# Two of the three split operand forms of the channel mixer kept unsplit in HBM, their parts made after loading

## The chip, the cores and the metric

The kernel runs on 1 core of one Trainium2 chip. The metric is the device time of one execution in microseconds (us); for the kernel before it is 2160.81 us, the median of 3 runs (2160.64 to 2161.2). Products of TensorE take float32 operands that are written as a sum of two parts, "hi" (rounded to the type fp32r) and "lo" (the rest, also fp32r); each product is hi x hi + hi x lo + lo x hi.

## The reference, cut to what matters

The kernel computes one step of a one-layer encoder (an RG-LRU branch and an mLSTM branch, merged, then a channel mixer) for 1024 prompt columns and 64 sample columns, so 1088 columns. The change touches only the channel mixer:

```python
hmlp = jax.nn.relu(rmsnorm(x, norm_mlp) @ w_up)      # D_MODEL 1024 -> D_FF 4096
x = x + (hmlp * hmlp) @ w_down                       # D_FF 4096 -> D_MODEL 1024
```

## The kernel before, in words

The first two thirds of the program (to about 1449 us) are the branches and their merge. The channel mixer follows. It is cut into **groups** of 1024 hidden rows: up groups 0 to 3 (normed x times w_up), then down groups 4, 5 and 6 (squared hidden rows of up groups 0, 1 and 2 times w_down); the hidden rows of up group 3 are multiplied at the very end by other code (`last_x`, `last_term`). Each group has 4 **units** (r = 0 to 3) of 256 output rows. Within a unit the 2 x 2 block product is made with 7 block products instead of 8 (Winograd's form of Strassen's method). The 7 operands on the x side are B11, T1, T2, B21, T3, B22, T4, each 512 rows x 544 columns; B are blocks of x, T are sums and differences of blocks. TensorE (`unit`, line 1184 on) takes the products in the order P5, P6, P2, P7, P1, P3, P4, whose operands are T1, T2, B21, T3, B11, B22, T4; the P1 in a unit is already that of the next unit. So at a change of group ("transition") B11 of the new group is wanted first, in the last unit of the old group, then T1, T2, B21, T3, B22, T4. "Half" below means two of an operand's four 128-row blocks; TensorE waits for operands that are made on the chip half by half (`by_pair`).

The operands of the down groups are made from hidden rows in the up groups and stored in HBM (`forms_d`). ScalarE squares two of a unit's four hidden quarters, VectorE the other two. VectorE then makes the three sums T1, T2, T4 (`hid_sums`, `last_sum`), ScalarE their hi parts (`sum_hi`), VectorE their lo parts in place (`sums_lo`), and `store` writes four quarters of B and T3, three lo parts and three hi parts with four DMAs from ScalarE's queue. So B11, T3, B21 and B22 are stored whole (list `RAW`), T1, T2 and T4 as hi and lo (list `SPLIT`).

At the end of groups 3, 4 and 5, and at the start of the next, the next group's operands are loaded into the same 7 operand buffers (`form[f][part]`), each as soon as TensorE has done the last product that reads the old contents. A whole form is one DMA (`load_raw`) of 1088 KB, after which ScalarE makes hi in two instructions (`raw_hi`) and VectorE makes lo in place in two (`raw_lo`); a split form is two DMAs (`load_split`) and nothing more. Before the change ScalarE's queue in the last unit (r = 3) runs: hi of B11 and the load of T1 after step 1, the load of T2 after step 2, of B21 after step 3, of T3 after step 4, hi of B21 and the load of B22 after step 6; and in unit 0 of the next group hi of T3, hi of B22 and the load of T4. A queue is in order: an instruction that waits holds all behind it.

Two other jobs share the queues there. ScalarE makes the hi part of each weight form (`w_form`) into one of 4 slots, once TensorE has done the product four before; GpSimd combines the weight blocks (`combine`, line 795) and makes the lo parts (`lo`, line 792), 11 instructions of 128 x 512 per unit, all of them from on-chip memory to on-chip memory. ScalarE copies P1 out of its bank (`copy1`, into `snap`). VectorE empties the other banks: `partials` (P6, P5), `quarter` and `direct` (P2, P7 twice, P3, P4), `mixed` adds a quarter to `acc` in groups 5 and 6. TensorE may start a product only when the bank four products back is empty: P7 of a unit waits for the P4 of the unit before to be emptied. In group 3 ScalarE's `relu2` on the quarter of P7 comes between `w_form` and the load of T3 (step 4), and VectorE's lo of B21 and T3 stand ahead of the emptying of P4 (`hid21`).

Of the kernel before, what the change touches and what calls it, by code (L numbers as in the profile page):

```python
# [137 lines left out]
RAW, SPLIT = (B11, B21, T3, B22), (T1, T2, T4)  # L138
# [30 lines left out]
STORED_HI = 3  # L169
KEPT = FORMS + 3  # L170
UNIT_STORES = 64
# [40 lines left out]
def build(nc, x_t, small_d, rowmask_d, w_d, c0_d, rows_d, mixa_d, y_d, conv_d, hlast_d, c_d, n_d, m_d):  # L212
# [114 lines left out]
    def quarters(t, first, n):  # L327
# [5 lines left out]
    hid_h = [(quarters(acc_flat, 3 + 9 * j, 2), quarters(stage[:].rearrange("p a c -> p (a c)"), 4 + j, 1))  # L333
             for j in range(2)]
# [971 lines left out]
    def _(act):  # L1306
# [418 lines left out]
        def store(group, r):  # L1725

            act.wait_ge(h_step, FORMS * (4 * group + r) + 7)
            th, t_hi2 = hid_h[r % 2]
            for src, first, n in ((hid_q[r % 2], 0, 4), (hid_t[r % 2], 4, 3), (th, 7, 2), (t_hi2, 9, 1)):
                dst = forms_d[bass.ds(KEPT * group + first, n)][:, :, r, :]  # L1730
                act.dma_start(dst.rearrange("f p c -> p f c"), src).then_inc(h_st[r % 2], 16)
# [16 lines left out]
        def sum_hi(group, r, i):  # L1748

            u, (th, t_hi2) = 4 * group + r, hid_h[r % 2]  # L1750
            if i == 0:
                for stored_hid, count in hid_free(group, r):
                    act.wait_ge(stored_hid, count)
            act.wait_ge(h_step, FORMS * u + (1, 3, 4)[i])
            a((th[:, i, :] if i < 2 else t_hi2[:, 0, :]).bitcast(F32R), hid_t[r % 2][:, i, :], ACT.Copy, h_hi)
# [110 lines left out]
        def hid(group, r, prev, late_sums=(1, 2, 3)):  # L1866

            def between(step):
                if step in late_sums[0:3]:
                    for i in range(3):  # L1870
                        if late_sums[i] == step:
                            sum_hi(*prev, i)
                if step == 4:
                    relu2(group, r, 0)
                    relu2(group, r, 1)
                elif step == 5 and isinstance(group, int) and group == 0 and r in (1, 2):
                    norm_out(r)
                elif step == 6:
                    store(*prev)
            return between  # L1880
        for r in range(1, 4):
            unit(0, r, hid(0, r, (0, r - 1), (1, 2, 3)))
# [23 lines left out]
        def operands(group, r, step):  # L1906

            v = group - UP_GROUPS + 2
            if v <= DOWN_GROUPS:
                if (r, step) == (2, 5):  # L1910
                    load_raw(v, 0)
                elif (r, step) == (3, 1):
                    raw_hi(v, 0)
                    act.wait_ge(s_mm, index(group, r, P5) + 1)
                    load_split(v, T1)
                elif (r, step) == (3, 2):
                    act.wait_ge(s_mm, index(group, r, P6) + 1)
                    load_split(v, T2)
                elif (r, step) == (3, 3):
                    act.wait_ge(s_mm, index(group, r, P2) + 1)  # L1920
                    load_raw(v, 1)
                elif (r, step) == (3, 4):
                    act.wait_ge(s_mm, index(group, r, P7) + 1)
                    load_raw(v, 2)
                elif (r, step) == (3, 6):
                    raw_hi(v, 1)
                    act.wait_ge(s_mm, index(group, r, P3) + 1)
                    load_raw(v, 3)
# [19 lines left out]
            if (r, step) == (0, 0) and v > 1:  # L1948
                raw_hi(v - 1, 2)
            if (r, step) == (0, 1) and v > 1:  # L1950
                raw_hi(v - 1, 3)
# [43 lines left out]
    def _(dve):  # L1995
# [609 lines left out]
        def hid_sums(group, r):  # L2605
# [7 lines left out]
            dve.wait_ge(h_step, FORMS * u + 1)  # L2613
            dve.wait_ge(h_sq, 4 * u + 4)
            hid_combine(q[1], q[3], q[1], ALU.subtract)
            dve.wait_ge(h_step, FORMS * u + 2)
            hid_combine(t[:, 1, :], q[1], q[0], ALU.add)

        def last_sum(group, r):
# [3 lines left out]
            dve.wait_ge(h_step, FORMS * u + 3)  # L2623
            hid_combine(t[:, 2, :], q[2], t[:, 1, :], ALU.subtract)

        def sums_lo(group, r):
            u, t, (th, t_hi2) = 4 * group + r, hid_t[r % 2], hid_h[r % 2]
            dve.wait_ge(h_step, FORMS * u + 4)
# [77 lines left out]
        for r in range(4):  # L2706
# [40 lines left out]
        for r in range(4):  # L2747
# [229 lines left out]
```

## Time and profile before

| | us |
|---|---|
| median of 3 runs | 2160.81 |
| lowest and highest | 2160.64 to 2161.2 |
| the profiled execution, its own time | 2157.67 |
| its span (first to last instruction) | 2155.8 |
| TensorE busy in the span | 2131.1 |
| VectorE, GpSimd, ScalarE busy | 1449.4, 1098.7, 717.1 |
| HBM read and written in the span | 171.86 MB and 64.16 MB |

The profile is of one execution; its times count from the start of the span. The granted TensorE clock was 0.997 over the span. Transition 1 (group 3 to 4) lies at about 1770 to 1805 us, transition 2 (4 to 5) at 1857 to 1890, transition 3 (5 to 6) at 1941 to 1976.

### The profile page before, as it was taken

The numbers are of one execution on the slowest core, as the hardware profiler recorded it, in microseconds if no ns is written. First come the engines' busy times: TensorE is split into PE (matmuls) and PEld (weight loads), VectorE is DVE, ScalarE is ACT, GpSimd is POOL, SyncE is SP. The second block draws the span as 40 slices with busy tenths as digits, with TensorE's granted clock in tenths as the row PEclk, the third lists the DMA queues.
The fourth block names the chain that finished last, engine by engine and source line by source line (L and its number), as shares of the span: only waits on it lengthen the run. The fifth ranks groups of instructions, "written<-read, shape, count | busy, mean of one in ns | idle before, by whom it ended". The sixth has DMA issues, their size and how long they took to land.

```text
span 2155.8 us, 37511 instructions
## 1 busy us (share of the span) xinstructions
PE 2131.1 (99%) x14270; PEld 2106.8 (98%) x14270; DVE 1449.4 (67%) x1525; ACT 717.1 (33%) x948; POOL 1098.7 (51%) x767
## 2 busy tenths in 40 slices
PE   9999999999999999999999999999999999999997
PEld 8999999999999999999999999999999999999987
DVE  7676776247767575857676756578877745367886
ACT  5443444213232322323232311234444433323332
POOL 4556554332424242424334245448787767687740
PEclk9999999999999999999999999999999999999999
DMA  3211212431212121211212123465455457536522
GB/s 129 71 58 56 69 54 91 149 109 52 69 43 70 46 73 53 61 59 49 62 45 67 44 95 97 148 222 181 175 189 199 160 180 263 209 112 262 182 65 83
DMA packets 98065, 237.18 MB, mean 110 GB/s; under 512 B 10656, under 2 KB 16928, under 8 KB 93120
## 3 DMA queue, kind: packets, MB, share of 16 engines
q1 hardware_dynamic: 59456, 109.52, 16.7%
q10 hardware_dynamic: 38528, 126.55, 16.0%
q8 instruction: 56, 0.92, 0.2%
q14 instruction: 25, 0.20, 0.0%
HBM read 171.86 MB, written 64.16 MB: 109 GB/s over the span
## 4 chain that ended last, share of the span: by engine, by line
PE 93%; DMA 2%; DVE 2%; ACT 1%; POOL 1%; issue 1%; SPq 0%; POOLq 0%; DVEq 0%; ACTq 0%
PE ps L902 56%; PE ps L1168 24%; PE ps L1265 4%; PE ps L1078 2%; PE ps L1111 2%; PE ps L1114 1%; PE ps L1093 1%; DMA form_lo<-hid_forms 1%; DMA last_x<-hid 1%; PE ps L1119 1%; PE ps L1065 1%; DVE p L2002 1%; DVE form_lo L2002 0%; PE ps L1066 0%; ACT vt L1548 0%
## 5 line engine op out<-in xcount | busy, mean ns | idle before, releaser
L763 POOL TENSOR_TENSOR w_hi<-w_raw,ones 128x512 fp32r<-128x512 f32 x216 | 261.7, 1211 | 815.1 <-PE ps L902 771.8
L766 POOL TENSOR_TENSOR w_lo<-w_raw,w_hi 128x512 fp32r<-128x512 f32 x216 | 335.7, 1554 | 16.9
L902 PE MATMUL ps<-u_hi,w_hi 128*128 128x364 f32 x1533 | 341.5, 331 | 2.2 <-DVE u_lo L1999 1.9
L902 PE MATMUL ps<-u_hi,w_lo 128*128 128x364 f32 x1533 | 338.5, 329 | 0.0
L902 PE MATMUL ps<-u_lo,w_hi 128*128 128x364 f32 x1533 | 338.3, 329 | 0.0
L902 PEld LDWEIGHTS ps<-u_hi,w_hi 128*128 128x128 f32 x1533 | 266.3, 188 | 4.1 <-DVE u_lo L1999 2.5
L902 PEld LDWEIGHTS ps<-u_lo,w_hi 128*128 128x128 f32 x1533 | 267.0, 188 | 0.0
L902 PEld LDWEIGHTS ps<-u_hi,w_lo 128*128 128x128 f32 x1533 | 266.8, 188 | 0.0
L1168 PE MATMUL ps<-form_hi,w_hi 128*128 128x272 f32 x776 | 161.4, 289 | 2.7 <-DVE acc L2002 2.0
L1168 PE MATMUL ps<-form_hi,hi 128*128 128x272 f32 x784 | 162.0, 288 | 0.4 <-POOL lo L792 0.4
L1168 PE MATMUL ps<-form_hi,lo 128*128 128x272 f32 x784 | 162.3, 288 | 0.0
L1168 PE MATMUL ps<-form_lo,hi 128*128 128x272 f32 x784 | 161.9, 288 | 0.0
L1168 PE MATMUL ps<-form_lo,w_hi 128*128 128x272 f32 x776 | 160.5, 288 | 0.0
L1168 PE MATMUL ps<-form_hi,w_lo 128*128 128x272 f32 x776 | 160.3, 288 | 0.0
L2002 DVE TENSOR_TENSOR acc<-acc 128x1092 f32<-128x1092 f32 (+2 forms) x72 | 111.4, 1560 | 33.4 <-ACT acc L1353 24.5
L1168 PEld LDWEIGHTS ps<-form_hi,w_hi 128*128 128x128 f32 x776 | 121.6, 188 | 4.1 <-DVE acc L2002 2.2
L1168 PEld LDWEIGHTS ps<-form_hi,hi 128*128 128x128 f32 x784 | 122.8, 188 | 0.6 <-POOL lo L792 0.6
L1168 PEld LDWEIGHTS ps<-form_hi,lo 128*128 128x128 f32 x784 | 122.8, 188 | 0.0
L1168 PEld LDWEIGHTS ps<-form_lo,hi 128*128 128x128 f32 x784 | 122.7, 188 | 0.0
L1168 PEld LDWEIGHTS ps<-form_lo,w_hi 128*128 128x128 f32 x776 | 121.9, 188 | 0.0
L1168 PEld LDWEIGHTS ps<-form_hi,w_lo 128*128 128x128 f32 x776 | 121.5, 188 | 0.0
L2002 DVE TENSOR_TENSOR acc<-ps,acc 128x1092 f32<-128x1092 f32 x64 | 82.2, 1285 | 11.6 <-PE ps L902 11.6
(341 smaller groups left out, 4489.1 us busy)
## 6 DMA issues: line engine op xcount, KB each, us to landing
w_raw<-in_w SPq DMA_DIRECT2D x280, 256.0 KB, 2.6
form_lo<-hid_forms ACTq DMA_DIRECT2D x21, 1088.0 KB, 9.8
rstd<-in_w SPq DMA_DIRECT2D x50, 256.0 KB, 2.7
hid_forms<-acc ACTq DMA_DIRECT2D x12, 816.0 KB, 6.0
form_hi<-hid_forms ACTq DMA_DIRECT2D x9, 1088.0 KB, 7.3
bc<-out_rows ACTq DMA_DIRECT2D x8, 1092.0 KB, 6.1
hid_forms<-stage ACTq DMA_DIRECT2D x6, 1088.0 KB, 4.5
hid_forms<-acc ACTq DMA_DIRECT2D x12, 544.0 KB, 6.9
```

The source lines that it names most:

```text
L763: nc.gpsimd.tensor_tensor(w_hi[:, c, :], w_raw[:, c, :], one, ALU.mult).then_inc(s_whi, 1)
L766: nc.gpsimd.tensor_tensor(w_lo[:, c, :], w_raw[:, c, :], w_hi[:, c, :].bitcast(F32), ALU.subtract).then_inc(s_wlo, 1)
L902: mm = nc.tensor.matmul(slots[slot][:, t, :], w, r(k)[:, t * TW:(t + 1) * TW], start=(k == 0 and n == 0), stop=(k == last_k and n == 2))
L1065: nc.tensor.matmul(ps[:, 6 + c % 2, 0:n], kz[:, k0:k0 + CH], preq[:, t0:t0 + n], start=True, stop=True)
L1078: mm = nc.tensor.matmul(out, l, r, start=(cb == 0 and n == 0), stop=(cb == 1 and n == 2))
L1093: nc.tensor.matmul(ps[:, c % 2, 0:VW], kt[:, c % 2, :], vt3[:, c, :], start=True, stop=True).then_inc(m_u_mm, 1)
L1111: nc.tensor.matmul(out, vt3[:, c, j * P:(j + 1) * P], sw[:, c % 2, 0:n], start=True, stop=state is None)
L1114: nc.tensor.matmul(out, state[:, j * P:(j + 1) * P], bc[:, 1, t0:t0 + n], start=False, stop=True)
L1119: nc.tensor.matmul(ps[:, 3 + c % 2, 2 * P:2 * P + n], ones[:], (zw if c else sw)[:, c % 2, 0:n], start=True, stop=True).then_inc(m_o_mm, 1)
L1168: mm = nc.tensor.matmul(out[:, t, :], l, x[:, k, t * HT:(t + 1) * HT], start=(k == 0 and n == 0), stop=(k == 3 and n == 2))
L1265: return nc.tensor.matmul(ps[:, q % LAST_BANKS, 0:hi - lo], w, last_x[:, k, int(term == 2), lo:hi], start=first, stop=last)
L2002: V.tensor_tensor(out, in0, in1, op).then_inc(inc, 1)
```

## The change

T1 and T2 move from `SPLIT` to `RAW`. In the up groups their hi and lo parts are no longer made; a unit is stored with 3 DMAs and 8 quarters where there were 4 DMAs and 10 quarters. At each of the three transitions T1 and T2 are loaded with one DMA each where there were two, their hi parts are made by ScalarE after steps 3 and 4 of the last unit (hi of B21 stays after step 6), and their lo parts by VectorE: T1's between the emptying of P2 and of P7, T2's between that of P7 and of P3. T4 stays split.

```diff
-RAW, SPLIT = (B11, B21, T3, B22), (T1, T2, T4)
+RAW, SPLIT = (B11, T1, T2, B21, T3, B22), (T4,)
...
-UNIT_STORES = 64
+UNIT_STORES = 48
...
         def store(group, r):
-            act.wait_ge(h_step, FORMS * (4 * group + r) + 7)
-            th, t_hi2 = hid_h[r % 2]
-            for src, first, n in ((hid_q[r % 2], 0, 4), (hid_t[r % 2], 4, 3), (th, 7, 2), (t_hi2, 9, 1)):
+            act.wait_ge(h_step, STEPS * (4 * group + r) + STEPS)
+            for src, first, n in ((hid_q[r % 2], 0, 4), (hid_t[r % 2], 4, 3), (hid_h[r % 2], 7, 1)):
...
-            for part in range(2):
-                src = forms_d[KEPT * (v - 1) + STORED[f] + (0 if part else STORED_HI)]
...
-                if step in late_sums[0:3]:
-                    for i in range(3):
-                        if late_sums[i] == step:
-                            sum_hi(*prev, i)
+                if step == 3:
+                    sum_hi(*prev)
...
                 elif (r, step) == (3, 1):
                     raw_hi(v, 0)
                     act.wait_ge(s_mm, index(group, r, P5) + 1)
-                    load_split(v, T1)
+                    load_raw(v, 1)
                 elif (r, step) == (3, 2):
                     act.wait_ge(s_mm, index(group, r, P6) + 1)
-                    load_split(v, T2)
+                    load_raw(v, 2)
                 elif (r, step) == (3, 3):
+                    raw_hi(v, 1)
                     act.wait_ge(s_mm, index(group, r, P2) + 1)
-                    load_raw(v, 1)
+                    load_raw(v, 3)
                 elif (r, step) == (3, 4):
+                    raw_hi(v, 2)
                     act.wait_ge(s_mm, index(group, r, P7) + 1)
-                    load_raw(v, 2)
+                    load_raw(v, 4)
                 elif (r, step) == (3, 6):
-                    raw_hi(v, 1)
+                    raw_hi(v, 3)
...
-            for i in range(3):
-                dve.wait_ge(h_hi, 3 * u + i + 1)
-                hid_combine(t[:, i, :].bitcast(F32R), t[:, i, :], th[:, i, :] if i < 2 else t_hi2[:, 0, :],
-                            ALU.subtract)
+            dve.wait_ge(h_hi, u + 1)
+            hid_combine(t[:, 2, :].bitcast(F32R), t[:, 2, :], high_part[:, 0, :], ALU.subtract)
...
-                f = {(3, 1): B11, (3, 4): B21, (3, 5): T3}.get((r, step))
+                f = {(3, 1): B11, (3, 2): T1, (3, 3): T2, (3, 4): B21, (3, 5): T3}.get((r, step))
...
             quarter(group, r, P2, q[0], snap1[:], 2)
+            operands(group, r, 2)
             quarter(group, r, P7, q[3], snap4, 2)
             quarter(group, r, P7, snap2[:], snap2[:], 1)
+            operands(group, r, 3)
```

(The last two additions stand in the loop of group 3 and again in that of group 4; group 5 had the calls already.)

Where VectorE's instructions stand at transition 3, in the last unit of group 5. `snap` and `small` rows that read `ps` empty banks, `acc<-acc` rows are `mixed`. The program before:

```order
L2002 TENSOR_TENSOR form_lo<-form_lo,form_hi 128x1088 x2
L2002 TENSOR_TENSOR snap<-ps,snap 128x544
L2002 TENSOR_TENSOR acc<-acc,snap 128x544
L2002 TENSOR_TENSOR snap<-ps,small 128x544
L2002 TENSOR_TENSOR snap<-ps,snap 128x544
L2002 TENSOR_TENSOR acc<-acc,snap 128x544
L2002 TENSOR_TENSOR small<-ps,small 128x544
L2002 TENSOR_TENSOR acc<-acc,small 128x544
L2002 TENSOR_TENSOR form_lo<-form_lo,form_hi 128x1088 x2
```

The same place in the changed program:

```order
L2000 TENSOR_TENSOR form_lo<-form_lo,form_hi 128x1088 x2
L2000 TENSOR_TENSOR snap<-ps,snap 128x544
L2000 TENSOR_TENSOR acc<-acc,snap 128x544
L2000 TENSOR_TENSOR form_lo<-form_lo,form_hi 128x1088 x2
L2000 TENSOR_TENSOR snap<-ps,small 128x544
L2000 TENSOR_TENSOR snap<-ps,snap 128x544
L2000 TENSOR_TENSOR acc<-acc,snap 128x544
L2000 TENSOR_TENSOR form_lo<-form_lo,form_hi 128x1088 x2
L2000 TENSOR_TENSOR small<-ps,small 128x544
L2000 TENSOR_TENSOR acc<-acc,small 128x544
L2000 TENSOR_TENSOR form_lo<-form_lo,form_hi 128x1088 x2
```

The pairs of T1 and T2 now stand between those of B11 and B21, each ahead of a bank's emptying.

ScalarE at transition 1, right after the load of T2 (last unit of group 3; `w_hi` and `hi` rows are weight forms, the row of four is `relu2`). The program before:

```order
L1308 ACTIVATE w_hi<-raw 128x512
L1763 DMA form_lo<-hid_forms 128x2176
L1308 ACTIVATE w_hi<-wsum 128x512
L1308 ACTIVATE acc<-acc 128x544 x4
L1763 DMA form_lo<-hid_forms 128x2176
L1308 ACTIVATE snap<-ps 128x544
L1308 ACTIVATE hi<-wsum 128x512
L1308 ACTIVATE hi<-w_raw 128x512
L1308 ACTIVATE form_hi<-form_lo 128x1088 x2
```

The same place in the changed program:

```order
L1308 ACTIVATE w_hi<-raw 128x512
L1308 ACTIVATE form_hi<-form_lo 128x1088 x2
L1761 DMA form_lo<-hid_forms 128x2176
L1308 ACTIVATE w_hi<-wsum 128x512
L1308 ACTIVATE acc<-acc 128x544 x4
L1308 ACTIVATE form_hi<-form_lo 128x1088 x2
L1761 DMA form_lo<-hid_forms 128x2176
L1308 ACTIVATE snap<-ps 128x544
L1308 ACTIVATE hi<-wsum 128x512
L1308 ACTIVATE hi<-w_raw 128x512
L1308 ACTIVATE form_hi<-form_lo 128x1088 x2
```

The hi parts of T1 and T2 now stand ahead of the loads of B21 and T3, and that of T2 also ahead of the copy of P1 and of the next two weight forms.

## Rows read from the trace of the kernel before

**Rows 1.** Page, part 1: engine, busy us, share, instructions.
```profile
PE 2131.1 (99%) x14270; PEld 2106.8 (98%) x14270; DVE 1449.4 (67%) x1525; ACT 717.1 (33%) x948; POOL 1098.7 (51%) x767
```
**Rows 2.** TensorE's waits over the span: us in total, times, longest.
```profile
PE ps L1168 <- DVE acc L2002: 2.0, 1, 2.0
...
PE ps L1168 <- DVE form_lo L2002: 0.7, 2, 0.5
PE ps L1168 <- POOL lo L792: 0.4, 1, 0.4
```
**Rows 3.** Window without transition stalls: busy us (instructions) of PE, PEld, DVE, ACT, POOL.
```profile
1835.00:1930.00 95.00, 95.00 (x759) 95.00 (x759) 46.57 (x48) 30.17 (x44) 70.41 (x50) 1.00 0.46 168
```
**Rows 4.** ScalarE timeline, transition 1: start, us, what, idle before.
```profile
1783.34 2.58 ACT L1308 ACTIVATE acc<-acc 128x544 f32<-128x544 f32 x4
...
1793.76 1.11 ACT L1308 ACTIVATE form_hi<-form_lo 128x1088 fp32r<-128x1088 f32 x1 [4.30 <-DMA form_lo<-hid_forms]
...
1796.64 2.11 ACT L1308 ACTIVATE form_hi<-form_lo 128x1088 fp32r<-128x1088 f32 x2 [0.24 <-DMA form_lo<-hid_forms]
```
**Rows 5.** VectorE timeline, transition 1.
```profile
1778.24 3.99 DVE L2002 TENSOR_TENSOR form_lo<-form_lo,form_hi 128x1088 fp32r<-128x1088 f32 x2
1782.15 0.71 DVE L2002 TENSOR_TENSOR acc<-ps,snap 128x544 f32<-128x544 f32 x1
...
1794.91 2.49 DVE L2002 TENSOR_TENSOR form_lo<-form_lo,form_hi 128x1088 fp32r<-128x1088 f32 x2 [3.50 <-ACT form_hi L1308]
1797.79 4.23 DVE L2002 TENSOR_TENSOR form_lo<-form_lo,form_hi 128x1088 fp32r<-128x1088 f32 x2 [0.38 <-ACT form_hi L1308]
1801.94 0.71 DVE L2002 TENSOR_TENSOR acc<-ps,snap 128x544 f32<-128x544 f32 x1
```
**Rows 6.** TensorE timeline, transition 1 and transition 3.
```profile
1802.71 0.52 PE L1168 MATMUL ps<-form_hi,w_hi 128*128 128x272 f32 x2 [1.96 <-DVE acc L2002]
...
1971.76 0.48 PE L1168 MATMUL ps<-form_hi,w_hi 128*128 128x272 f32 x2 [0.20 <-DVE form_lo L2002]
...
1973.97 0.52 PE L1168 MATMUL ps<-form_hi,w_hi 128*128 128x272 f32 x2 [0.46 <-DVE form_lo L2002]
```
**Rows 7.** GpSimd timeline, transition 1.
```profile
1779.05 2.02 POOL L795 TENSOR_TENSOR wsum<-rstd 128x512 f32<-128x512 f32 x1 [0.28 <-POOL lo L792]
1781.04 2.35 POOL L792 TENSOR_TENSOR w_lo<-raw,w_hi 128x512 fp32r<-128x512 f32 x1
1783.35 1.30 POOL L795 TENSOR_TENSOR rstd<-w_raw,rstd 128x512 f32<-128x512 f32 x1
```
**Rows 8.** Tile form_lo: durations ns min/median/max of one; then its DMAs.
```profile
L1308 ACT ACTIVATE form_hi<-form_lo x24: 1092/1098/1117, 1774.3 to 1971.5; 128x1088 fp32r<-128x1088 f32 x24
L2002 DVE TENSOR_TENSOR form_lo<-form_lo,form_hi x24: 1281/1716/2386, 1778.2 to 1977.5; 128x1088 fp32r<-128x1088 f32 x24
...
DMA to landing us min/median/max: 5.4/9.7/14.2
```
**Rows 9.** Window in transition 1: as rows 3, the last three are clock, DMA share, GB/s.
```profile
1785.00:1790.00 5.00, 5.00 (x42) 5.00 (x41) 1.14 (x2) 2.77 (x5) 3.94 (x4) 1.00 1.01 421
```
**Rows 10.** VectorE timeline, transition 3.
```profile
1953.71 1.07 DVE L2002 TENSOR_TENSOR acc<-acc,snap 128x544 f32<-128x544 f32 x1
...
1956.09 1.68 DVE L2002 TENSOR_TENSOR acc<-acc,snap 128x544 f32<-128x544 f32 x1
...
1966.05 2.50 DVE L2002 TENSOR_TENSOR form_lo<-form_lo,form_hi 128x1088 fp32r<-128x1088 f32 x2 [4.51 <-ACT form_hi L1308]
...
1970.32 3.59 DVE L2002 TENSOR_TENSOR form_lo<-form_lo,form_hi 128x1088 fp32r<-128x1088 f32 x2
...
1975.29 4.59 DVE L2002 TENSOR_TENSOR form_lo<-form_lo,form_hi 128x1088 fp32r<-128x1088 f32 x2
```
**Rows 11.** VectorE timeline, transition 2: the emptying of P2.
```profile
1868.67 0.71 DVE L2002 TENSOR_TENSOR acc<-ps,snap 128x544 f32<-128x544 f32 x1
```
**Rows 12.** ScalarE's queue of DMA issues, transition 2: T1's load, at the end of P5.
```profile
1860.45 0.35 ACTq L1772 DMA_DIRECT2D form_hi<-hid_forms  x1
```

More of the change, by code:

```diff
@@ L168 @@
 STORED = {B11: 0, T3: 1, B21: 2, B22: 3, T1: 4, T2: 5, T4: 6}
-STORED_HI = 3
-KEPT = FORMS + 3
-UNIT_STORES = 64
+STORED_HI = {T4: 7}
+KEPT = FORMS + len(SPLIT)
+STEPS = 4 + len(SPLIT)
+UNIT_STORES = 48
 FORMS_STORED = 2 * UNIT_STORES * (GROUPS - 1)
@@ L332, in build @@
     hid_t = [quarters(acc_flat, 0, 3), quarters(acc_flat, 9, 3)]
-    hid_h = [(quarters(acc_flat, 3 + 9 * j, 2), quarters(stage[:].rearrange("p a c -> p (a c)"), 4 + j, 1))
-             for j in range(2)]
+    hid_h = [quarters(acc_flat, 3 + 9 * j, 1) for j in range(2)]
     raw11, raw12, raw21 = w_raw[:, 0, :], w_raw[:, 1, :], rstd[:, 0:CHUNK]
@@ L1746, in relu2, with sum_hi @@
             a(ap, ap, ACT.Square, h_sq)
[L1748 to L1755, printed above, removed]
+        def sum_hi(group, r):
+            u = 4 * group + r
+            for stored_hid, count in hid_free(group, r):
+                act.wait_ge(stored_hid, count)
+            act.wait_ge(h_step, STEPS * u + 4)
+            a(hid_h[r % 2][:, 0, :].bitcast(F32R), hid_t[r % 2][:, 2, :], ACT.Copy, h_hi)
         def load_raw(v, i):
@@ L1770, in load_split @@
             for part in range(2):
-                src = forms_d[KEPT * (v - 1) + STORED[f] + (0 if part else STORED_HI)]
+                src = forms_d[KEPT * (v - 1) + (STORED[f] if part else STORED_HI[f])]
                 act.dma_start(form[f][part][:].bitcast(F32), src).then_inc(done, 16)
@@ L1864, in _, with hid @@
         w_form(0, 1, P2, raw12)
-        def hid(group, r, prev, late_sums=(1, 2, 3)):
+        def hid(group, r, prev):
             def between(step):
-                if step in late_sums[0:3]:
-                    for i in range(3):
-                        if late_sums[i] == step:
-                            sum_hi(*prev, i)
+                if step == 3:
+                    sum_hi(*prev)
                 if step == 4:
@@ L1881, in _ @@
         for r in range(1, 4):
-            unit(0, r, hid(0, r, (0, r - 1), (1, 2, 3)))
+            unit(0, r, hid(0, r, (0, r - 1)))
         def up_group(group):
@@ L1948, in operands @@
             if (r, step) == (0, 0) and v > 1:
-                raw_hi(v - 1, 2)
+                raw_hi(v - 1, 4)
             if (r, step) == (0, 1) and v > 1:
-                raw_hi(v - 1, 3)
+                raw_hi(v - 1, 5)
                 act.wait_ge(s_mm, index(group, r, P5))
@@ L2612, in hid_sums @@
             hid_combine(t[:, 0, :], q[1], q[0], ALU.subtract)
-            dve.wait_ge(h_step, FORMS * u + 1)
+            dve.wait_ge(h_step, STEPS * u + 1)
             dve.wait_ge(h_sq, 4 * u + 4)
             hid_combine(q[1], q[3], q[1], ALU.subtract)
-            dve.wait_ge(h_step, FORMS * u + 2)
+            dve.wait_ge(h_step, STEPS * u + 2)
             hid_combine(t[:, 1, :], q[1], q[0], ALU.add)
@@ L2622, in last_sum @@
             dve.wait_ge(h_sqv, 2 * u + 2)
-            dve.wait_ge(h_step, FORMS * u + 3)
+            dve.wait_ge(h_step, STEPS * u + 3)
             hid_combine(t[:, 2, :], q[2], t[:, 1, :], ALU.subtract)
         def sums_lo(group, r):
-            u, t, (th, t_hi2) = 4 * group + r, hid_t[r % 2], hid_h[r % 2]
-            dve.wait_ge(h_step, FORMS * u + 4)
-            for i in range(3):
-                dve.wait_ge(h_hi, 3 * u + i + 1)
-                hid_combine(t[:, i, :].bitcast(F32R), t[:, i, :], th[:, i, :] if i < 2 else t_hi2[:, 0, :],
-                            ALU.subtract)
+            u, t, high_part = 4 * group + r, hid_t[r % 2], hid_h[r % 2]
+            dve.wait_ge(h_step, STEPS * u + 4)
+            dve.wait_ge(h_hi, u + 1)
+            hid_combine(t[:, 2, :].bitcast(F32R), t[:, 2, :], high_part[:, 0, :], ALU.subtract)
         def up_unit(group, r, prev, extra=None):
@@ L2753, in _ @@
             direct(group, r, P2, 2 * r, 0, snap1[:], 2, 0)
+            operands(group, r, 2)
             direct(group, r, P7, 2 * r + 1, 1, snap4, 2, 0)
             quarter(group, r, P7, snap2[:], snap2[:], 1)
+            operands(group, r, 3)
             direct(group, r, P3, 2 * r, 1, snap4, 2, 3)
```

2 lines of the change are left out of this document (1 added, 1 removed).

## The prediction

> **What bounds the kernel now.** I read the page's first part, then TensorE's waits, then the timelines of the three transitions. TensorE is busy 2131.1 of 2155.8 us, VectorE only 1449.4 [rows 1]: only what makes TensorE wait, or wait less, changes the time. In the channel mixer the whole list of its waits is 2.0 + 0.7 + 0.4 us [rows 2]. The 0.4 is at the mixer's start, which the change doesn't touch. In the window without a wait, 759 matmuls take 95.00 us [rows 3], so a product (24 matmuls) takes 3.00 us and a half of one 1.5 us. The change gives TensorE the same matmuls.
>
> The 2.0 us: at transition 1 P7 of group 4's first unit starts at 1802.71 after 1.96 us idle, so its due time is 1800.75 [rows 6]. It waited for VectorE's emptying of P4, which ran at 1801.94, behind the lo parts of B21 (1794.91) and T3 (1797.79, 4.23 us) [rows 5]. Those were late because ScalarE, which makes the hi parts, waited for loads: 4.30 us for B21, until 1793.76, then for T3 until 1796.64 [rows 4]. The loads were late because the DMA engines were full: in the window inside the stretch their share is 1.01 at 421 GB/s [rows 9]. The 0.7 us: at transition 3 P7 waits 0.20 us for the first and 0.46 us for the second half of T3's lo part [rows 6], again VectorE behind a load, where it idles 4.51 us [rows 10].
>
> So before a transition's end VectorE is idle for a while because of loads, and then is what TensorE waits for. The change shortens the loads and gives VectorE more to do.
>
> **What a lo instruction costs.** One lo half takes from 1281 to 2386 ns, median 1716 [rows 8]. The spread is GpSimd. The B21 pair at 1794.91 took 2.49 us, while the T3 pair took 4.23 and B11's 3.99 [rows 5]; during B11's, GpSimd ran instructions of 2.02 and 2.35 us, and the next, with VectorE on a bank read, took 1.30 [rows 7]. A VectorE instruction from on-chip memory with two such inputs and a GpSimd instruction take turns, and each waits for the other; those that read a bank (0.71 us) stay short [rows 5]. A pair costs 2.5 us with GpSimd idle. With GpSimd busy the rows have 3.6 (transition 3's T3) to 4.6 [rows 10], and twice the longest half would be 4.8. GpSimd is busy 70.41 of 95 us [rows 3], and more pairs make its queue denser, since it loses time to them too. I take **4.4** for a pair in dense stretches, nearest to 4.23 and 4.59, and keep 3.6 and 4.8 as the ends.
>
> The Trainium skill (SBUF — State Buffer, section Who interferes with whom) says that the pair of ports is locked for a whole instruction and the loser fully blocks. By that a half could cost its own time plus a whole GpSimd instruction each time, some 2.6 us, a pair 5.2 (an estimate from the page's rule), and the sum would lie above my upper end; the longest half seen, 2386 ns [rows 8], is less.
>
> **The change part by part.**
>
> *Up groups.* 24 hi copies on ScalarE, 24 lo subtractions on VectorE and 12 DMAs go. TensorE waits for none of this [rows 2]: 0 us. Nor is there a loss, since no wait is added.
>
> *Loads.* Two of the six DMAs up to T3's are gone at each transition, 2.2 MB, at 421 GB/s 5.3 us. The loads then keep up: alone a form lands in 5.4 us [rows 8], so T1 is there when ScalarE comes to it, and B21's load is issued at once. By itself this would take both waits away, 2.7 us in all. That is the most that the change can gain.
>
> *ScalarE.* Four hi instructions of 1.10 us [rows 8] per transition. T2's two stand ahead of the load of T3, the copy of P1 and two weight forms. ScalarE is busy a third of the time (30.17 of 95 us [rows 3]); I walk it where it counts.
>
> *VectorE.* Four lo halves per transition, 8.8 us by my price, into about the 4.5 us of idle time seen. The walk, on due times of TensorE:
>
> Transition 1. P2 is emptied at 1782.86 [rows 5]. T1's pair 4.4: 1787.3. Two emptyings of P7, 1.4: 1788.7. ScalarE's second relu and square must wait for the first of these (1788.0) and take half of 2.58 [rows 4]: 1789.3; then T2's hi halves, 1790.4 and 1791.5. T2's lo, GpSimd meanwhile short of weight forms: 1.28 after the last hi, 1792.8. P3's emptying and VectorE's own square, 0.7 + 1.1: 1794.6. B21 4.4: 1799.0. T3 4.4: 1803.4. P4 emptied 1804.1, due 1800.75: a wait of 3.35 for 1.96, **+1.4**. With 3.6 a pair: 1801.6, -1.1. With 4.8 (T2's too, and a longer square): 1808.3, +5.6.
>
> Transition 2. ScalarE has no relu there, and in groups 4 and 5 P4 is emptied before T3's lo. P5 ends at 1860.45 [rows 12], so nine products later P7 is due at 1887.5. P2 is emptied at 1869.4 [rows 11]. With three pairs (13.2), P7 (1.4), P3 and P4 (0.7 each) VectorE is at 1885.4, T3's halves are done at 1887.6 and 1889.8: waits of 0.1 and 0.7. GpSimd isn't busy all of that time; I take half, **+0.4** (ends 0 and 2.4).
>
> Transition 3. Here `mixed` adds 1.07 to 1.68 us three times [rows 10], as they too take turns with GpSimd. VectorE is done with P2 at 1954.8. T1 4.4: 1959.2; P7 1.4: 1960.6; mixed 1.7: 1962.3; T2, half of it against GpSimd, 3.4: 1965.7; P3 and mixed 1.8: 1967.5. B21's halves: 1969.7 and 1971.9. T3's P7 is due at 1971.56 [rows 6], so P2, which reads B21, at 1968.55: waits of 1.15 and 0.7. P4 and mixed 1.8: 1973.7. T3's halves: 1975.9 and 1978.1; TensorE would come at 1973.4: waits of 2.5 and 0.7. In all 5.05 for 0.66, **+4.4** (3.6 a pair: 1.1 of waits, +0.4; 4.8: 8.8, +8.1).
>
> Sum: 1.4 + 0.4 + 4.4 = **+6.2 us** (ends -0.7 and +16.1). The profiled execution took 2157.67 us (span 2155.8), so 2163.9; the median of the runs is 3.1 us above it, and moves with it: 2160.81 + 6.2 = **2167.0 us**. After each transition VectorE has idle time again and TensorE's wait is not made good.
>
> **The rivals.** A measurement of this kernel can tell a change from none from about 0.2% on, 4.3 us.
>
> *The lighter loads pay for it (not slower).* VectorE's waits for loads (3.50 us at transition 1 [rows 5], 4.51 at transition 3 [rows 10]) are filled with the new pairs, T3 comes earlier, and the pairs are cheap as the T3 pair of 3.59 at transition 3 was. It decides at a price per pair of about 3.6, where the sum crosses 0: -0.7, **2160.1 us**; up to 4.1 a pair the time stays within 4.3 us. For it: the DMA engines are full now. Against it: GpSimd has enough queued to take a turn after every lo half. The Trainium skill (SBUF — State Buffer, section A bandwidth-pool intuition that's wrong) holds that HBM is almost always the end-to-end bottleneck; by that fewer bytes would give the 2.7 us of waits back, 2158.1. No row shows TensorE short of bytes for longer.
>
> *GpSimd becomes late as well.* Its weight parts are made late, since T2's hi holds two weight forms on ScalarE (to about 1792.5 at transition 1) and every lo half costs GpSimd a turn. From there it has P6's lo, P2's lo, a combination and P7's lo to make: four at 2.35 [rows 7] end at 1802, still ahead of VectorE's 1804. If it is later by 2 to 3 us at two transitions, and then at the products after, this adds some 6 us: **2173 us**. For it: both queues wait for each other. Against: in the rows GpSimd idles for some time in each unit.
>
> **How the numbers follow.** My forecast 0.63 (0.60 of it above 2165.1), lighter loads 0.27, GpSimd late 0.10. The range 2161.0 to 2172.5 leaves out about 0.1 on each side: below, the cheap pairs with a real gain; above, the ends at 4.8. Faster by over 0.2% would need more than the 2.7 us that there are to gain: 0.02. Within 0.2%: 0.28. Slower: 0.70.
>
> **What would show it.** Right: TensorE waits at transitions 1 and 3 grow to about 3 and 5 us, with VectorE (form_lo, or the emptying of P4) as releaser; ScalarE's waits for loads at the transitions nearly vanish; the median lo half rises from 1716 ns to 2 us or more; no wait at all in the up groups. At transition 3 some of it falls on P2 (B21) already. Wrong: TensorE's waits stay at 3 us or less in all (then the rival of the loads), or they name weight parts of GpSimd (the other), or ScalarE still waits for loads.

## The result, and the profile after

The changed kernel takes **2163.96 us** (median of 22 runs, 2161.24 to 2166.38). Run beside it, the kernel before takes 2161.06 us (22 runs, 2155.63 to 2164.92). The ratio is 1.0018 with a 95% interval of 1.0012 to 1.0024, so by the ratio the change costs about 3.9 us (2.6 to 5.2); the two medians by themselves are 2.9 us apart. That is slower, and by either number less than the bound of 0.2% (4.3 us), though the interval reaches past it. The forecast was 2167.0, inside a range of 2161.0 to 2172.5.

The profiled execution took 2163.96 us, as much as the median, with a span of 2161.8. The first part of its page answers to [rows 1]:

```profile
PE 2132.9 (99%) x14270; PEld 2108.8 (98%) x14270; DVE 1440.9 (67%) x1513; ACT 713.2 (33%) x936; POOL 1104.6 (51%) x767
```

TensorE has the same 14270 matmuls but is busy 1.8 us longer. HBM traffic fell from 171.86 MB read and 64.16 written to 165.18 and 57.48.

TensorE's waits over the span, as in [rows 2] (us in total, times, longest):

```profile
PE ps L1168 <- DVE acc L2000: 3.3, 1, 3.3
PE ps L902 <- POOL w_lo L766: 2.9, 2, 2.6
...
PE ps L1168 <- DVE form_lo L2000: 2.5, 2, 2.3
...
PE ps L1168 <- POOL lo L792: 0.4, 1, 0.4
```

The same two waits have grown: 3.3 for 2.0 at transition 1, 2.5 for 0.7 at transition 3. The second line belongs to the program's first part (2.9 us before as well) and is needed further down. TensorE's timeline at the two transitions, as in [rows 6]:

```profile
1803.72 0.82 PE L1168 MATMUL ps<-form_hi,w_hi 128*128 128x272 f32 x2 [3.27 <-DVE acc L2000]
...
1972.68 0.51 PE L1168 MATMUL ps<-form_hi,hi 128*128 128x272 f32 x2 [0.17 <-DVE form_lo L2000]
...
1976.78 0.49 PE L1168 MATMUL ps<-form_hi,w_hi 128*128 128x272 f32 x2 [2.33 <-DVE form_lo L2000]
```

P7 waits for VectorE's emptying of P4 (3.27 us), then, at transition 3, P2 waits a little for B21 (0.17) and P7 2.33 us for the first half of T3. At transition 2 there is no wait. The lo parts and the loads, as in [rows 8]:

```profile
L2000 DVE TENSOR_TENSOR form_lo<-form_lo,form_hi x36: 1275/2275/2398, 1777.9 to 1982.4; 128x1088 fp32r<-128x1088 f32 x36
...
DMA to landing us min/median/max: 5.2/7.2/10.9
```

There are 36 lo halves instead of 24, and the median half is 2275 ns for 1716, while the lowest and highest are nearly as before. A load lands after 7.2 us in the median, for 9.7. VectorE's timeline at transition 1, as in [rows 5]:

```profile
1777.95 3.98 DVE L2000 TENSOR_TENSOR form_lo<-form_lo,form_hi 128x1088 fp32r<-128x1088 f32 x2
1781.86 0.71 DVE L2000 TENSOR_TENSOR acc<-ps,snap 128x544 f32<-128x544 f32 x1
1782.49 4.06 DVE L2000 TENSOR_TENSOR form_lo<-form_lo,form_hi 128x1088 fp32r<-128x1088 f32 x2
...
1789.61 2.49 DVE L2000 TENSOR_TENSOR form_lo<-form_lo,form_hi 128x1088 fp32r<-128x1088 f32 x2 [1.79 <-ACT form_hi L1308]
...
1793.77 9.27 DVE L2000 TENSOR_TENSOR form_lo<-form_lo,form_hi 128x1088 fp32r<-128x1088 f32 x4
1802.96 0.71 DVE L2000 TENSOR_TENSOR acc<-ps,snap 128x544 f32<-128x544 f32 x1
```

These are the pairs of B11, T1 (4.06), T2 (2.49), then B21 and T3 in one row of four halves (9.27, so 4.6 a pair), then the emptying of P4, 1.02 us later than before. VectorE still idles 1.79 us ahead of T2's pair, but B21's and T3's come back to back: the 3.50 us of idle time ahead of B21's pair [rows 5] is gone. At transition 3, as in [rows 10]:

```profile
1957.27 4.57 DVE L2000 TENSOR_TENSOR form_lo<-form_lo,form_hi 128x1088 fp32r<-128x1088 f32 x2
...
1963.03 0.71 DVE L2000 TENSOR_TENSOR acc<-acc,snap 128x544 f32<-128x544 f32 x1
1963.77 2.49 DVE L2000 TENSOR_TENSOR form_lo<-form_lo,form_hi 128x1088 fp32r<-128x1088 f32 x2
...
1968.04 4.58 DVE L2000 TENSOR_TENSOR form_lo<-form_lo,form_hi 128x1088 fp32r<-128x1088 f32 x2
...
1974.40 4.53 DVE L2000 TENSOR_TENSOR form_lo<-form_lo,form_hi 128x1088 fp32r<-128x1088 f32 x2
```

T1's, B21's and T3's pairs cost 4.5 to 4.6; T2's fell into a pause of GpSimd's and cost 2.49, and so did the `mixed` ahead of it (0.71).

**Something else shows.** The two spans differ by 6.0 us (2155.8 and 2161.8), but the waits in the mixer by only 3.1. The rest is in the granted clock. Windows of 2 us right behind the wait at transition 1, after (columns as in [rows 3]):

```profile
1804.00:1806.00 2.00, 2.00 (x10) 2.00 (x11) 1.90 (x3) 0.00 (x0) 0.16 (x1) 0.50 0.50 191
1806.00:1808.00 2.00, 2.00 (x15) 2.00 (x15) 2.00 (x3) 0.00 (x0) 1.58 (x1) 0.84 0.01 5
...
1978.00:1980.00 2.00, 2.00 (x11) 2.00 (x10) 1.90 (x3) 0.00 (x0) 1.50 (x1) 0.50 1.00 410
```

and the first of them in the trace of before:

```profile
1804.00:1806.00 2.00, 2.00 (x18) 2.00 (x18) 1.90 (x4) 0.00 (x0) 1.74 (x2) 1.00 0.99 413
```

At each of the two long waits TensorE's clock falls to 0.50 (1.2 of 2.4 GHz) for 3.4 us: from 1803.2 on, half a microsecond before the first wait ends, and from 1977.3 on, half a microsecond after the second. Behind the waits TensorE is busy all the time, and its windows hold 10 or 11 matmuls where the one of before, at full clock, holds 18. The price can be read from VectorE rows that TensorE paces. Before:

```profile
1815.06 0.72 DVE L2002 TENSOR_TENSOR acc<-ps,snap 128x544 f32<-128x544 f32 x1 [2.28 <-PE ps L1168]
...
1947.70 0.72 DVE L2002 TENSOR_TENSOR snap<-ps,snap 128x544 f32<-128x544 f32 x1 [3.53 <-PE ps L1168]
...
1993.85 0.72 DVE L2002 TENSOR_TENSOR snap<-ps,snap 128x544 f32<-128x544 f32 x1 [1.29 <-PE ps L1168]
```

The same three after:

```profile
1817.38 0.72 DVE L2000 TENSOR_TENSOR acc<-ps,snap 128x544 f32<-128x544 f32 x1 [2.28 <-PE ps L1168]
...
1950.14 0.72 DVE L2000 TENSOR_TENSOR snap<-ps,snap 128x544 f32<-128x544 f32 x1 [3.53 <-PE ps L1168]
...
1999.65 0.72 DVE L2000 TENSOR_TENSOR snap<-ps,snap 128x544 f32<-128x544 f32 x1 [1.29 <-PE ps L1168]
```

P7 at transition 1 starts 1.01 us later than before (1803.72, 1802.71), and the first row comes 2.32 later: 1.31 us went in the slow stretch. From the second row to the third it is 46.15 us before and 49.51 after, 3.36 more. The waits in between grew by 1.84 (2.50 for 0.66), which leaves 1.52 for the second slow stretch. Together 2.8 us, nearly as much as the waits themselves grew. Ahead of transition 1 the changed execution is 0.3 us early, and about as much is lost in small pieces behind it, which makes up the 6.0 us.

### The profile page after: what moved, and what is told of

It reads as the page before. It is cut to its first block, busy times and chain, and to the rows that moved or that the text cites. A ratio compares the mean times of both kernels' runs of the same rounds, so it can differ in the third digit from the quotient of the medians.

```text
span 2161.8 us, 37445 instructions
## 1 busy us (share of the span) xinstructions
PE 2132.9 (99%) x14270; PEld 2108.8 (98%) x14270; DVE 1440.9 (67%) x1513; ACT 713.2 (33%) x936; POOL 1104.6 (51%) x767
## 3 DMA queue, kind: packets, MB, share of 16 engines
HBM read 165.18 MB, written 57.48 MB: 103 GB/s over the span
## 4 chain that ended last, share of the span: by engine, by line
PE 93%; DVE 3%; DMA 1%; issue 1%; ACT 1%; POOL 1%; SPq 0%; DVEq 0%; POOLq 0%; ACTq 0%
PE ps L902 56%; PE ps L1168 24%; PE ps L1265 4%; PE ps L1078 2%; PE ps L1111 2%; PE ps L1114 1%; PE ps L1093 1%; DMA last_x<-hid 1%; DVE form_lo L2000 1%; PE ps L1119 1%; PE ps L1065 1%; DVE p L2000 1%; DVE acc L2000 0%; PE ps L1066 0%; ACT vt L1548 0%
## 5 line engine op out<-in xcount | busy, mean ns | idle before, releaser
L2000 DVE TENSOR_TENSOR acc<-acc 128x1092 f32<-128x1092 f32 (+2 forms) x60 | 93.8, 1564 | 60.4 <-ACT acc L1308 33.8
```

Source lines behind the costliest of these rows:

```text
L2000: V.tensor_tensor(out, in0, in1, op).then_inc(inc, 1)
```

## The experiments

Eight kernels ran, in two groups on one chip each, and are compared with the kernel before run beside them (2160.72 us for the first four, 2160.18 for the next four); then the kernels before and after were traced twice more. The changed kernel was not run beside the eight. Where a run is set against its 2163.96 us, the comparison goes across groups, in which the kernel before alone differs by up to 0.9 us.

### Is it the loads that made the kernel before wait?

Before, with the hi parts of T1 and T2 not loaded but for one block's 64 columns:

```diff
+                dst = form[f][part][:].bitcast(F32)
+                if f != T4 and part == 0:
+                    src, dst = src[:, 0:1, 0:64], dst[:, 0:1, 0:64]
```

> The program before, with the hi parts of T1 and T2 not loaded but for a sliver of 64 columns of one block (the products of groups 4 to 6 read stale hi parts there, so less is transferred and nothing else changes). Theory 1 (before, loads made VectorE late; now VectorE's own queue does): TensorE's waits at transitions 1 and 3, 1.96 and 0.66 us, are both gone, no 1.2 GHz stretch there, 2.7 to 4 us faster than before. Rival (the loads never mattered, VectorE's order of work does): waits stay at 2.0 and 0.7, time unchanged.

2154.51 us, ratio 0.9977 (0.9967 to 0.9986), span 2152.1. TensorE has no wait at any transition. So the loads cause both waits, but the gain is 5 us by the ratio and 6.2 by the medians, above the 2.7 to 4 expected: it is more than the profiled execution of before had to give. Why is settled by the two traces of before below.

The changed kernel with T1 and T2 loaded once more each, into the hi buffer (ScalarE waits for both loads before it makes the hi part there):

```diff
+            if f in (T1, T2):
+                act.dma_start(form[f][0][:].bitcast(F32), forms_d[KEPT * (v - 1) + STORED[f]])\
+                    .then_inc(e_xy if f == T1 else e_zs, 16)
```

> The changed program, with T1 and T2 each loaded a second time, into their hi buffers, before ScalarE writes the hi parts over it: as many transfers as before the change, and the work of the change on top. Theory 1: the new pairs start later, waits at transitions 1 and 3 grow from 3.3 and 2.5 to about 5 and 4, some 3 to 5 us slower than the changed program (about 3 to 4 if loads only shift what VectorE waits for). Rival (VectorE is full anyway, so loads are hidden): waits unchanged, 5.8 us in all.

2169.3 us (four runs), ratio 1.0044 (1.0027 to 1.006), 5.3 us above the changed kernel. Its waits at the transitions:

```profile
PE ps L1168 <- issue: 4.1, 3, 1.8
PE ps L1168 <- DVE acc L2005: 3.4, 1, 3.4
PE ps L1168 <- DVE form_lo L2005: 3.4, 4, 2.3
```

The 4.1 us (1.80 at transition 1, 1.53 and 0.72 at transition 2) have no releaser in the trace. The waits for VectorE are within 1 us of those of the changed kernel, so neither the theory (5 and 4 us) nor its rival (nothing grows) foresaw where the loss shows. The slow stretch at transition 1 is 6.8 us long instead of 3.4, and at transition 3 there is none, though the wait there is 2.33 us as in the changed kernel. So the lighter loads are worth some 5 us to the changed kernel, and the pairs take more than that back.

### Is it VectorE's time, and is it the turns with GpSimd?

The changed kernel with T1's and T2's lo parts made for 32 of 544 columns only, TensorE's work being the same:

```diff
+                if f in (T1, T2):
+                    hi, lo = hi[:, :, 0:32], lo[:, :, 0:32]
                 tt(lo, lo.bitcast(F32), hi.bitcast(F32), ALU.subtract, s_nlo)
```

> The changed program, with VectorE's lo instructions of T1 and T2 cut to 32 of 544 columns (the rest of these lo parts is left as loaded, so less is computed). Theory 1 (VectorE's time is what costs): the waits at both transitions fall under 0.5 us, no 1.2 GHz stretch there, and the time is that of e1, about 3 us under before and 6 under the changed program. Rival (ScalarE's order costs: T2's hi ahead of the load of T3 and of the weight forms): waits of 2 us or more stay at transition 1.

2154.85 us, ratio 0.9974 (0.9964 to 0.9984), span 2151.8, no wait at any transition. That is some 9 us below the changed kernel: about the 6 us that the light loads gave to the kernel before, and the 3 that the change costs. ScalarE's hi parts and their place ahead of the loads are all still there, so by themselves they cost nothing that can be seen; the loss is VectorE's time in the two pairs.

The changed kernel with GpSimd's combinations and lo parts of groups 3 to 6 cut to 32 of 512 columns, as many instructions:

```diff
+            cols = slice(0, 32 if narrow[0] else CHUNK)
+            nc.gpsimd.tensor_tensor(w_los[s][:, cols], src[:, cols], w_his[s].bitcast(F32)[:, cols],
+                                    ALU.subtract).then_inc(v_lo, 1)
```

> The changed program, with GpSimd's instructions in groups 3 to 6 cut to 32 of 512 columns (the rest of the weight sums and lo parts is stale, so less is computed). Theory 1 (turns with GpSimd make a lo half 2.3 us instead of 1.28): every lo half takes 1.3 us, no wait at the transitions, about as fast as e3. Rival (the halves are long for another reason, such as the transfers that write on-chip memory): the median half stays at 2.2 us or so, waits stay near 5.8 us.

2154.74 us, ratio 0.9974 (0.9963 to 0.9985). The lo halves, and two of GpSimd's instructions:

```profile
L2009 DVE TENSOR_TENSOR form_lo<-form_lo,form_hi x36: 1280/1285/1343, 1778.3 to 1969.2; 128x1088 fp32r<-128x1088 f32 x36
```

```profile
1777.59 0.25 POOL L795 TENSOR_TENSOR lo<-wsum,hi 128x32 fp32r<-128x32 f32 x1 [2.74 <-ACT hi L1317]
1777.92 0.25 POOL L801 TENSOR_TENSOR wsum<-rstd 128x32 f32<-128x32 f32 x1
```

All 36 halves now take 1.28 us, and no wait is left at the transitions. The spread from 1.28 to 2.40 us is GpSimd's doing. It is not that of the loads: with the light loads of the first run the median half took 2372 ns. Alone, a half takes 1.28 and a GpSimd instruction 1.30 [rows 7]; in turns each takes 2.3 to 2.4, a little less than the sum of both.

The Trainium skill (SBUF — State Buffer, section Who interferes with whom) says that a `tensor_tensor` with both inputs in SBUF contends with GpSimd's reads for a shared pair of ports, held exclusively. This run agrees: 1285 ns in the median against 2275. That the holder keeps the pair for a whole instruction and the other fully blocks, the same section states of VectorE's 2-port modes, not of `tensor_tensor`. So the 5.2 us a pair that the prediction estimated from it does not follow for this instruction, and the longest half after the change took 2398 ns, 4.8 us a pair.

### Does the slow clock follow the long wait?

The changed kernel with 16 matmuls more (128 x 240, into a part of the bank that nobody reads) behind P2 in the first unit of groups 4 and 6, where TensorE otherwise stands still:

```diff
+            if isinstance(group, int) and group in (UP_GROUPS, UP_GROUPS + 2) and r == 0 and product == P2:
+                for _ in range(16):
+                    mm = nc.tensor.matmul(ps[:, 2 * s, HT:BANK], form[f][0][:, 0, 0:P], form[f][0][:, 0, 0:BANK - HT],
+                                          start=True, stop=True)
```

> The changed program, with 16 matmuls of 128 x 240 that nobody reads, into spare columns of P2's bank, put right behind P2 of the first unit of groups 4 and 6, where TensorE then waits 3.3 and 2.3 us for VectorE. They take some 1.8 us each time, inside the wait. Theory 2 (each long wait is followed by about 3.4 us at 1.2 GHz, which costs as much again as the wait's excess): the waits seen fall to about 1.5 and 0.5 us, both slow-clock stretches go, and the time falls by 2 to 3.4 us against the changed program, to about 2161. Rival (the clock has nothing to do with the wait): slow stretches stay, time unchanged at 2164 or 1 to 2 us more, as P2's result is signalled later.

2162.02 us, ratio 1.0006 (0.9996 to 1.0015), for the 1.0018 of the change: about 2 us back, with more work. The two intervals just touch, so the times alone are weak evidence; the traces (table below) show 2.0 to 2.4 us as well. The waits, and TensorE at transition 1:

```profile
PE ps L1168 <- DVE acc L2004: 1.5, 1, 1.5
PE ps L1168 <- DVE form_lo L2004: 1.2, 3, 0.6
```

```profile
1804.00:1806.00 2.00, 2.00 (x18) 2.00 (x18) 1.90 (x3) 0.00 (x0) 0.65 (x2) 1.00 0.58 223
```

P7 starts at 1803.71, as in the changed kernel (1803.72): VectorE was no earlier. But the idle time in front of it is 1.50 us and not 3.27, the clock stays at 1.00, and there are 18 matmuls in the window for 10. At transition 3 P7 now waits for both halves of T3 (0.56 and 0.46 us). In the changed kernel TensorE, at half clock there, took so long over the first half that the second was never late: a part of the slow clock's cost stands in for a wait.

### Can the waits be taken away by order?

The changed kernel with P4 emptied ahead of T3's lo parts in group 3, and `mixed` behind them in groups 5 and 6:

```diff
             operands(group, r, 4)
+            if r == 3:
+                dve.wait_ge(h_sq, 4 * u + 4)
+                quarter(group, 3, P4, q[2], snap2[:], 5)
             operands(group, r, 5)
...
+                if not final:
+                    operands(group, r, 5)
                 mixed(u, part2, 0, 2 * r + 1, 7, 4)
```

> The changed program with two moves in VectorE's queue: at the end of group 3 the bank of P4 is emptied before T3's lo halves and not after; in groups 5 and 6 the last addition of a unit (mixed) comes after those halves. The work is the same. Theory 1: transition 1's wait falls from 3.3 to about 1.5 us (now for T3's lo halves), transition 3's from 2.5 to about 1.5; with one or no slow-clock stretch some 4 to 6 us less than the changed program, about 2159. Rival (the length of VectorE's queue alone counts): waits stay over 2.5 and 2 us.

2161.07 us, ratio 0.9998 (0.9989 to 1.0007), 2.9 below the changed kernel. Its waits between 1750 and 2000 us:

```profile
PE ps L1168 <- DVE small L2000: 2.9, 2, 1.5
PE ps L1168 <- DVE form_lo L2000: 2.1, 5, 0.6
```

They sum to 5.0 us, little less than 5.8. What VectorE owes is the same; the order only moves TensorE's wait to what is next in VectorE's queue (`partials`, the bank that P1 needs). But it now comes in seven pieces of at most 1.5 us, and the clock is 1.00 at all transitions. Of the 2.3 us between this trace and the changed kernel's (table below) the waits are 0.8, so most of the gain is the clock's. The expectation of about 2159 us, with transition 1's wait down to 1.5, missed: at transition 1 it is 2.3 us in three pieces (0.45, 0.46 and 1.42).

The same order in the kernel before:

> The program before with the same two moves as e6. Theory 1: transition 1's wait falls from 2.0 to under 0.7 us, transition 3's from 0.7 to under 0.2, no slow-clock stretch at either; 3 to 6 us faster than before, about 2156. Rival (the load of T3 sets it, not the order): 1.5 us or more stay at transition 1, less than 2 us gained.

2158.62 us, ratio 0.9991 (0.998 to 1.0002), not told apart from before; 3 to 6 us had been expected, and 1.6 by the medians came. Transition 1 has no wait, transition 3 has 0.28 and 0.45, and T4's load costs 1.46 us, which the expectation had not counted.

T1 alone unsplit, T2 left split, in this order, with B21's load ahead of T1's hi parts in ScalarE's queue:

```diff
-RAW, SPLIT = (B11, T1, T2, B21, T3, B22), (T4,)
+RAW, SPLIT = (B11, T1, B21, T3, B22), (T2, T4)
```

> Only T1 is stored and loaded unsplit, T2 and T4 stay split, with the two moves of e6, and B21's load is issued ahead of T1's hi. Theory 1 (there is room in VectorE's queue for one pair, and one load less brings B21 and T3 forward by 2.7 us): no wait at transition 1, 0.5 to 1.5 us at transition 3, about 2156 to 2158, between e6 and e7 or level with e7. Rival (fewer bytes pay): faster than e7 by over 1 us.

2158.42 us, ratio 0.9989 (0.9979 to 0.9999): 5.5 us below the change, at most just faster than the kernel before, and level with the one above that has the new order alone. Its waits at the transitions sum to 2.1 us (1.8 of them `partials`). So with one form unsplit the lighter load and the new pair about cancel; no gain of its own could be shown.

### How much do the traces of one kernel differ?

The kernel before, traced twice more:

> The program before, unchanged, profiled once more. Theory 2 (a long wait may be followed by a slow-clock stretch, and usually is when it is about 2 us or more): the wait at transition 1 is again 2.0 us, and if the time is near the median of 2161 rather than 2157.7, a slow-clock stretch follows it or the wait of 2.5 us at 490 us. Rival: no slow stretch but the one at the start, and a time near 2161 with the same waits, so that the spread has another cause.

> As e9, one more look at the same program: the wait at transition 1 stays at 2.0 us, and the time goes with the number of slow-clock stretches, some 1.5 us each.

2163.23 us (span 2161.3) and 2160.82 us (span 2158.9); a run of the same kernel beside them took 2157.15. The mixer's waits of the first:

```profile
PE ps L1168 <- DMA form_lo<-hid_forms: 2.5, 1, 2.5
PE ps L1168 <- DVE acc L2002: 2.0, 1, 2.0
...
PE ps L1168 <- DVE form_lo L2002: 0.5, 1, 0.5
PE ps L1168 <- POOL w_lo L792: 0.5, 1, 0.5
PE ps L1168 <- DMA form_lo<-late_forms: 0.4, 1, 0.4
...
```

and of the second:

```profile
PE ps L1168 <- DVE form_lo L2002: 1.6, 4, 0.5
PE ps L1168 <- DMA form_lo<-hid_forms: 1.6, 1, 1.6
PE ps L1168 <- DVE acc L2002: 1.2, 1, 1.2
...
```

With the 0.4 us at the mixer's start they sum to 6.3 and 4.8 us, for 3.1 in the profile from which the forecast was made [rows 2]. In both, T4's load, the last of transition 3, is late for TensorE by 2.5 and 1.6 us, a wait that the first trace doesn't have at all. The wait at transition 1, expected to stay at 2.0 us, was 2.05 and 1.20. The waits that the loads cause come and go between executions, and the first trace was a lucky one, 3.4 us below the median of the 22 runs.

The changed kernel, twice more:

> The changed kernel once more, to see which of its stalls recur from one execution to the next. If the slow stretches of TensorE (granted clock at its lower level, 3.41 us long) belong to the two waits at transitions 1 and 3, this execution shows them again behind waits of 3.3 and 2.5 us and takes about 2164 us (span 2162). If they fell there by chance, the waits are there and the slow stretches are not, and it takes about 2161 us. If the waits themselves vary as those of the kernel before do (4.4 and 5.9 us in all in its last two traces, for 2.7 in its first), their sum differs by 1 us or more from 5.8.

> The same kernel in a third traced execution, for the spread: waits at the transitions of 5.8 us in all and slow stretches behind both (about 2164 us) if they belong to the kernel; about 2161 us without the slow stretches.

2164.35 and 2165.35 us; a run of the kernel before beside them took 2158.08. Both have the same two lines for TensorE's waits, 3.3 and 2.5 us with a longest of 2.3, as the first trace, and a slow stretch at each wait, so both belong to the kernel. In the changed kernel the waits are the same to the tenth of a microsecond in three executions, since they come from VectorE's queue and not from transfers.

Two rows of VectorE that TensorE paces stand in every trace, one ahead of transition 1 (at 1761.67 us in before's first trace, at 1761.38 in after's) and one behind transition 3 (at 1993.85 and 1999.65, shown above). All three transitions lie between them:

| trace | between the rows, us | named waits there, us | slow clock there, us |
|---|---|---|---|
| light loads, short lo parts, narrow GpSimd | 228.8 (all three) | 0 | 0 |
| before, the first | 232.2 | 2.6 | 0 |
| before, traced twice more | 234.9, 235.0 | 5.0, 4.4 | 0 |
| after, three traces | 238.3, 238.7, 238.4 | 5.8 | 6.8 |
| after, filled | 236.2 | 2.7, and about 3.6 of filling | 0 |
| after, reordered | 236.0 | 5.0 | 0 |

The kernel before loses 3.4 us to its transitions in the first trace and 6.1 to 6.2 in the other two: that is why the light loads gained more than 2.7. A wait also costs more than the idle time that the trace names: 6.2 us for 4.4 in six pieces, 7.2 for 5.0 in seven, so some 0.3 us a piece (an estimate from these rows).

## Why the prediction was right, and where not

**Right: the sign and the mechanism.** The loads stop being late, VectorE becomes what TensorE waits for at transitions 1 and 3, and the price is GpSimd's turns. The median half rose to 2275 ns ("2 us or more"), the pairs in dense stretches cost 4.06 to 4.64 us (4.4 was taken), ScalarE's waits for loads fall from 14.3 us at the three transitions to 4.0 (1.06, 1.73 and 1.16, one at each), a small part of transition 3's wait falls on P2, and the up groups have no new wait. The size of the change, though, 3.9 us, is within the 0.2% to which the prediction gave 0.28 and not beyond it, where it put 0.70. The runs with light loads, short lo parts and narrow GpSimd instructions each take one cause away, and the waits go with it.

**Transition 1: right.** 3.27 us measured, 3.35 forecast (+1.3 for +1.4). Two of its terms were off and cancelled: T1's pair took 4.06 us for 4.4, and those of B21 and T3 together 9.27 for 8.8.

**Transition 2: 0 for +0.4.** The pairs took 3.6 to 4.1 us there, and VectorE was in time.

**Transition 3: mis-sized.** The term was 5.05 us of wait for 0.66, +4.4; it was 2.50, +1.8. Most of the difference is VectorE's queue, which was about 2 us shorter than in the walk: T2's pair was charged half a turn with GpSimd, 3.4 us (2.41 in the trace to the next row), and the `mixed` behind P7 1.7 (0.74). GpSimd had itself run dry there. Its timeline, and ScalarE's:

```profile
1960.77 2.23 POOL L795 TENSOR_TENSOR wsum<-wsum,w_raw 128x512 f32<-128x512 f32 x1
1965.05 2.37 POOL L792 TENSOR_TENSOR lo<-wsum,hi 128x512 fp32r<-128x512 f32 x1 [2.06 <-ACT hi L1308]
```

```profile
1963.83 0.62 ACT L1308 ACTIVATE snap<-ps 128x544 f32<-128x544 f32 x1 [4.24 <-DVE acc L2000]
```

GpSimd waits 2.06 us for a hi part of ScalarE's. ScalarE was not busy with T1's and T2's hi parts then: its copy of P1, which stands ahead of that weight form, had waited 4.24 us for VectorE to be done with `snap`, in the `mixed` behind T1's new pair. So the new work on VectorE held ScalarE, ScalarE held GpSimd, and VectorE's next instructions ran alone. That the queues starve each other was in the text for T2 at transition 1; at transition 3 it was allowed for by half at T2 and not at all at `mixed`. The rest of the difference is the 0.7 us for T3's second half, which the slow clock hid (the run with the filling shows it, 0.46).

**Not in the forecast: the clock.** No term stood for it. It costs 1.3 + 1.5 us, which happens to fill most of what the waits fell short of: +3.1 from waits and +2.8 from the clock, against a forecast of +6.2 from waits alone. Against the profiled execution of before (2157.67 + 6.2 = 2163.9) the sum looks exact at 2163.96, and that is luck in its parts.

**The step that failed against the median** is "the median of the runs is 3.1 us above it, and moves with it". It doesn't. In the execution of before at 2160.82 us, close to the median, 2.8 of the 3.1 us lie at the transitions (235.0 us between the two rows for 232.2), where late loads cause them, and the change takes those away: the changed kernel's profiled execution is its median. Between that execution and the changed one the spans differ by 2.9 us: waits +1.4 (6.2 for 4.8), slow clock +2.8, which together make 4.2. Most of the 1.3 us too much is the uncounted cost of a wait: before has six at the transitions and loses 1.8 us beyond their names, the changed kernel has three and loses 0.9 beyond waits and clock. The other 0.4 us stay open. For the same reason "the most that the change can gain", 2.7 us, was too low: with light loads the kernel gained 5 to 6.

**The rivals.** "The lighter loads pay for it" had its mechanism right (they are worth some 5 us), but the pairs in the dense stretches were not as cheap as the 3.6 us that it needed. With narrow GpSimd instructions (2.5 a pair) the same program is 6 us faster than before; at which price between 2.5 and 4.6 it would break even, no run shows. Its companion rule in the Trainium skill (SBUF — State Buffer, section A bandwidth-pool intuition that's wrong), that HBM is almost always the bottleneck, pointed to fewer bytes being a gain. By themselves they were one, but with TensorE busy for 99% of the span the VectorE work that paid for them cost more: 13.4 MB less moved, and the kernel is slower. "GpSimd becomes late as well" didn't happen: TensorE waits for it 0.4 us, as before.

## What to carry to other kernels

A saved transfer that is paid for with vector work must be priced by what the vector engine competes with at that place, not by the instruction alone: here one lo half costs 1.28 us beside an idle GpSimd and 2.3 to 2.4 beside a busy one. Before a forecast of a few microseconds, trace the old kernel more than once: a wait caused by transfers may be absent in the one execution at hand, and is then missing from what the change can win. And where a wait can't be removed, breaking it up (another order, or a few matmuls in it that nobody reads) can save the slow clock behind it: about 2 us here, of the 3 to 4 that the change costs.

## What the hardware showed that was not expected

A short wait can cost more than itself. In three executions of the changed kernel the waits of 3.27 and 2.33 us each brought 3.4 us at a granted clock of 0.50, worth 1.3 and 1.5 us in the one where the price was read. It is no function of the length of the wait alone. With the heavy loads a wait of 2.33 us at the same place brought none. In one trace of the kernel before, the waits are 2.53 us at transition 3 and 2.05 at transition 1, and the clock stays at 1.00 behind both:

```profile
1806.00:1808.00 2.00, 2.00 (x16) 2.00 (x17) 1.90 (x4) 2.00 (x4) 0.15 (x1) 1.00 0.92 261
```

(the window behind the wait of 2.05 us). The wait of 2.55 to 2.57 us for `w_lo` at about 490 us, in the program's first part, is followed by a slow stretch in the other two traces of before and not in the first. A wait of 1.8 us at about 40 us is followed by one in the first two traces of before and not in the third. The window 490 to 510 us in the first trace of before:

```profile
490.00:510.00 20.00, 17.23 (x126) 16.51 (x125) 14.59 (x28) 10.46 (x14) 6.95 (x6) 1.00 0.30 95
```

and in the third:

```profile
490.00:510.00 20.00, 17.83 (x119) 17.41 (x120) 11.86 (x27) 10.02 (x13) 7.57 (x6) 0.91 0.26 84
```

Same program, same wait, another clock. It is a part of why executions of one kernel differ: of the three traces of before, the one with both stretches reaches transition 1 about 3 us later than the two with one. What decides it was not found; no run here varied it by itself.
